# Two activation parts through one weight tile in 512 columns, with the halves added on VectorE

## The reference, cut to what matters

```
# first network, one layer
h = rms_norm(x, norm_pre_g)
proj = einsum('bsd,de->bse', h, w_in)       # q, k, u_a, z_a, o, z_b, g_a, g_b: 1024 columns each; v and gates apart
# second network, two layers; each ends with
def peer_ffn(h, w_q, sub_keys, u_tab, v_tab):
    q = (xc @ w_q).reshape(t, PEER_HEADS, 2, PEER_QDIM // 2)     # 2048 columns
    sc = einsum('thpc,hpnc->thpn', q, sub_keys)                  # then top-k, experts, sum
```

## Time and profile before

| | us |
|---|---|
| median of 3 runs (2314.62 to 2317.86) | 2315.11 |
| time of the profiled execution | 2312.29 |
| its span | 2310.5 |
| PE busy in the span | 2226.4 (96%) |
| DVE busy | 1700.3 (74%) |
| ACT busy | 1169.5 (51%) |

### The profile page before, as it was taken

One profiled execution on the slowest core, in us unless ns is written; L12 is line 12 of the kernel. 1 busy time (PEld: TensorE's weight loads), 2 busy tenths in 40 slices (PEclk: granted clock), 3 DMA queues, 4 the chain that ended last, 5 costly groups with the idle time before them and its releaser, 6 DMA issues.

```text
span 2310.5 us, 44458 instructions
## 1 busy us (share of the span) xinstructions
PE 2226.4 (96%) x15960; PEld 2011.1 (87%) x15960; DVE 1700.3 (74%) x3205; ACT 1169.5 (51%) x1688; POOL 0.2 (0%) x4
## 2 busy tenths in 40 slices
PE   7999899899999999999999998999999999999998
PEld 7998787689999999878888887899999998888886
DVE  5787676855998687798755567569977778986554
ACT  5566344545555555444444455545564554444444
POOL 0000000000000000000000000000000000000000
PEclk9999999799999999999999999999999999999999
DMA  6444244234545444455555542435554444555553
GB/s 262 178 180 152 92 149 149 73 107 149 177 169 190 156 168 168 146 172 173 183 190 190 191 153 79 155 137 173 181 179 158 172 165 149 178 166 190 190 190 137
DMA packets 95589, 376.37 MB, mean 163 GB/s; under 512 B 10861, under 2 KB 10989, under 8 KB 92817
## 3 DMA queue, kind: packets, MB, share of 16 engines
q1 hardware_dynamic: 95504, 375.29, 47.0%
HBM read 374.20 MB, written 1.05 MB: 162 GB/s over the span
## 4 chain that ended last, share of the span: by engine, by line
PE 70%; DVE 16%; ACT 2%; issue 2%; DMA 0%; ACTq 0%; SPq 0%; DVEq 0%
PE bank L328 21%; PE bank L330 21%; PE bank L329 21%; DVE tile_lo L2269 4%; PE bank L2003 3%; DVE e_hidden L2295 2%; DVE e_hidden L2289 2%; DVE e_hidden L2301 1%; DVE e_hidden L2341 1%; DVE e_hidden L2343 1%; DVE e_hidden L2339 1%; PE bank L2087 1%; DVE tile_lo L260 0%; PE bank L295 0%; PE bank L875 0%
## 5 line engine op out<-in xcount | busy, mean ns | idle before, releaser
L329 PE MATMUL bank<-a_lo,tile_hi 128*128 128x256 f32 x2688 | 756.1, 281 | 0.0
L328 PE MATMUL bank<-a_hi,tile_hi 128*128 128x256 f32 x2176 | 623.1, 286 | 16.4 <-DVE tile_lo L2269 5.3
L330 PE MATMUL bank<-a_hi,tile_lo 128*128 128x256 f32 x2176 | 613.7, 282 | 0.0
L329 PEld LDWEIGHTS bank<-a_lo,tile_hi 128*128 128x128 f32 x2688 | 511.4, 190 | 0.0
L2221 ACT ACTIVATE tile_hi<-wbuf 128x1024 fp32r<-128x1024 f32 x248 | 263.4, 1062 | 388.3 <-PE bank L330 385.4
L328 PEld LDWEIGHTS bank<-a_hi,tile_hi 128*128 128x128 f32 x2176 | 413.1, 190 | 24.1 <-issue 13.7
L2393 DVE TENSOR_TENSOR tile_lo<-wbuf,tile_hi 128x1024 fp32r<-128x1024 f32 x256 | 312.3, 1220 | 164.2 <-ACT tile_hi L2221 164.2
L330 PEld LDWEIGHTS bank<-a_hi,tile_lo 128*128 128x128 f32 x2176 | 413.3, 190 | 0.0
L328 PE MATMUL bank<-tile_hi,hidden_hi 128*128 128x512 f32 x1024 | 407.4, 398 | 5.0 <-DVE hidden_lo L2396 5.0
L330 PE MATMUL bank<-tile_hi,hidden_lo 128*128 128x512 f32 x1024 | 402.7, 393 | 0.0
L329 PE MATMUL bank<-tile_lo,hidden_hi 128*128 128x512 f32 x1024 | 402.4, 393 | 0.0
(11 more groups left out here) (355 smaller groups left out, 3112.6 us busy)
## 6 DMA issues: line engine op xcount, KB each, us to landing
wbuf<-in_peer_u SPq DMA_DIRECT2D x256, 512.0 KB, 3.5
wbuf<-in_peer_v SPq DMA_DIRECT2D x256, 512.0 KB, 3.5
wbuf<-in_w_in SPq DMA_DIRECT2D x16, 2048.0 KB, 7.7
wbuf<-in_peer_q SPq DMA_DIRECT2D x32, 512.0 KB, 4.0
wbuf<-in_hyb_in SPq DMA_DIRECT2D x16, 512.0 KB, 3.6
wbuf<-in_mla_uq SPq DMA_DIRECT2D x9, 512.0 KB, 3.5
wbuf<-in_mla_in SPq DMA_DIRECT2D x8, 528.0 KB, 3.3
wbuf<-in_w_v SPq DMA_DIRECT2D x2, 2048.0 KB, 7.2
```

The costliest lines, as they stand in the source:

```text
L328: nc.tensor.matmul(out, hi[:, cols], other_hi, start=start, stop=False, **kw)
L329: nc.tensor.matmul(out, hi[:, cols], other_lo, start=False, stop=False, **kw)
L330: return nc.tensor.matmul(out, lo[:, cols], other_hi, start=False, stop=stop, **kw)
```

## The change

In the input sections and the query projections a triple of matmuls becomes a pair. The two parts of the activations lie side by side (`n_parts`, `q_parts`, seen as 2 x 256 columns); `lo` of the weights goes with the high activations alone (256 columns), and `hi` of the weights with both parts in one matmul of 512 columns. The sum for an output tile now takes a whole bank: one half holds hi·hi + lo·hi, the other hi·lo. ACT copies the half with hi·lo out, and DVE adds the other half to it; DVE's addition is what frees the bank. In the input sections four banks are now used by groups of two, and groups alternate between two pairs of banks; in the query projections tile j uses bank 2 + j % 2, and PE waits for the kept tile j-2 before every tile from j = 2 on. `n_hi` moves to the buffer that was `a_hi`; eight semaphores are taken from the pool that is cleared and used again later. The core of it:

```
+def paired_products(nc, out, main, hi, lo, parts, other_hi, k, start, stop):
+    cols = slice(k * P, (k + 1) * P)
+    nc.tensor.matmul(out[:, main * S:(main + 1) * S], lo[:, cols], other_hi, start=start, stop=False, ...)
+    return nc.tensor.matmul(out, hi[:, cols], parts, start=False, stop=stop, skip_group_check=True)

 # input sections, PE (one triple becomes one pair; banks by twos)
-  last = three_products(nc, bank[:, b, e * S:(e + 1) * S], in_hi[:, slot, :], in_lo[:, slot, :],
-                        n_hi[:, k, :], n_lo[:, k, :], n, k == 0, k == KT - 1)
+  last = paired_products(nc, bank[:, 2 * (b % 2) + e, :], 1, in_hi[:, slot, :], in_lo[:, slot, :],
+                         n_parts[:, :, k, :], n_hi[:, k, :], n, k == 0, k == KT - 1)
 # ACT: starts bank_free at 2 instead of 4; after each group
-  nc.scalar.activation(proj[...2 tiles...], bank[:, b, :], ACT.Copy).then_inc(bank_free, 1)
+  nc.scalar.activation(proj[...2 tiles...], bank[:, 2 * (b % 2):2 * (b % 2) + 2, 0:S], ACT.Copy).then_inc(low_kept, 1)
 # DVE: after the rest of the piece that ACT rounds before that copy
+  def add_parts(i, b):
+      part = proj[:, bass.ds(i * KT + 2 * b, 2), :]
+      dve.wait_ge(low_kept, 4 * i + b + 1)
+      nc.vector.tensor_tensor(part, bank[:, 2 * (b % 2):2 * (b % 2) + 2, S:2 * S], part, ALU.add).then_inc(bank_free, 1)

 # query projections, PE
-  if j >= 4 and j % 2 == 0:
-      pe.wait_ge(q_kept, j // 2 - 1)
-  columns_product(nc, pe, g, M_Q + j, bank[:, 2 + j // 2 % 2, ...256 columns...], q_hi, q_lo, ...)
+  if j >= 2:
+      pe.wait_ge(q_kept, j - 1)
+  pe.wait_ge(lo_done, M_Q + j + 1)
+  for k in range(KT):
+      last = paired_products(nc, bank[:, 2 + j % 2, :], 0, tile_hi[:, slot, :], tile_lo[:, slot, :],
+                             q_parts[:, :, k, :], q_hi[:, k, :], k, k == 0, k == KT - 1)
 # ACT, per tile, ahead of round_tile(M_Q + j + SLOTS)
-  if j % 2:
-      nc.scalar.activation(q_T[...2 tiles...], bank[:, 2 + j // 2 % 2, :], ACT.Copy).then_inc(q_kept, 1)
+  act.wait_ge(used, M_Q + j + 1)
+  nc.scalar.activation(q_T[:, j, :], bank[:, 2 + j % 2, S:2 * S], ACT.Copy).then_inc(q_low, 1)
 # DVE
+  def keep_query(j):
+      dve.wait_ge(q_low, j + 1)
+      nc.vector.tensor_tensor(q_T[:, j, :], bank[:, 2 + j % 2, 0:S], q_T[:, j, :], ALU.add).then_inc(q_kept, 1)
   for j in range(HALVES - 1):
       ...
       rest_tile(nc, dve, g, M_Q + j + SLOTS)
+      keep_query(j)
+  keep_query(HALVES - 1)
```

More of the change, by code:

```diff
@@ L131, in build @@
         _, h_at = fixed("h_T", [P, KT, S])
-        _, other_at = fixed("h_other", [P, KT, S])
+        fixed("h_other", [P, KT, S])
         wbuf, wbuf_at = fixed("wbuf", [P, NW, SLOTS * TILE])
@@ L159, in build @@
             "tile_lo": rounded("tile_lo", [P, SLOTS, TILE], wbuf_at + 2 * BUF),
[L160 to L161 removed]
+            "a_parts": rounded("a_parts", [P, 2, KT, S], h_at),
             "hidden_hi": rounded("hidden_hi", [P, SLOTS, S], x_at),
@@ L170, in build @@
         }
+        g["a_lo"], g["a_hi"] = (g["a_parts"][:, part, :, :] for part in range(2))
         early = []
@@ L330, in three_products @@
     return nc.tensor.matmul(out, lo[:, cols], other_hi, start=False, stop=stop, **kw)
+def paired_products(nc, out, main, hi, lo, parts, other_hi, k, start, stop):
+    cols = slice(k * P, (k + 1) * P)
+    nc.tensor.matmul(out[:, main * S:(main + 1) * S], lo[:, cols], other_hi, start=start, stop=False, skip_group_check=True)
+    return nc.tensor.matmul(out, hi[:, cols], parts, start=False, stop=stop, skip_group_check=True)
 def first_layer(nc, g, ins):
@@ L343, in first_layer @@
         gate_hi, gate_lo = (g["rounded"](f"gate_{n}", [P, KT, GATES], sig_at + i * KT * GATES * 4) for i, n in enumerate(("hi", "lo")))
-        at = sb.at()
         v_one = sb("v_one", [P, NT, HEADS, HD + 1], stack=own)
-        n_hi, n_lo = g["rounded"]("n_hi", [P, KT, S], at), g["a_lo"]
+        n_hi, n_lo, n_parts = g["a_hi"], g["a_lo"], g["a_parts"]
         mix = sb("mix", [P, GROUPS, 2, 2 * P], stack=own)
@@ L517, in behind, with keep_low @@
                     if j % 4 == 3:
[L518 to L522, removed]
+                        keep_low(i, j // 4)
+                def keep_low(i, b):
+                    nc.scalar.activation(proj[:, bass.ds(i * KT + 2 * b, 2), :], bank[:, 2 * (b % 2):2 * (b % 2) + 2, 0:S],
+                                         ACT.Copy).then_inc(low_kept, 1)
                 act.wait_ge(g["in_loaded"][0], DMA)
@@ L712, in next_rest @@
                         rest(source, pieces % SLOTS_IN, pieces + 1)
+                        behind = pieces - SLOTS_IN
+                        if behind < PIECES * NSEC and behind % 4 == 3:
+                            add_parts(behind // PIECES, behind % PIECES // 4)
                         pieces += 1
@@ L1916, in expert_layer @@
     xn = flat(24, 32).rearrange("p (t d) -> p t d", t=NT)
-    q_hi, q_lo = (g["rounded"](f"{tag}_q_{n}", [P, KT, S], hidden_at + row * S * 4) for n, row in (("hi", 32), ("lo", 40)))
+    q_parts = g["rounded"](f"{tag}_q_parts", [P, 2, KT, S], hidden_at + 32 * S * 4)
+    q_hi, q_lo = (q_parts[:, part, :, :] for part in range(2))
     junk = flat(48, 56).rearrange("p (t d) -> p t d", t=NT)
@@ L2066, in tensor @@
         for j in range(HALVES):
-            if j >= 4 and j % 2 == 0:
-                pe.wait_ge(q_kept, j // 2 - 1)
-            columns_product(nc, pe, g, M_Q + j, bank[:, 2 + j // 2 % 2, (j % 2) * S:(j % 2 + 1) * S], q_hi, q_lo,
-                            None if j else parts_ready)
+            slot = (M_Q + j) % SLOTS
+            if j >= 2:
+                pe.wait_ge(q_kept, j - 1)
+            pe.wait_ge(lo_done, M_Q + j + 1)
+            for k in range(KT):
+                if j == 0:
+                    parts_ready(k)
+                last = paired_products(nc, bank[:, 2 + j % 2, :], 0, tile_hi[:, slot, :], tile_lo[:, slot, :],
+                                       q_parts[:, :, k, :], q_hi[:, k, :], k, k == 0, k == KT - 1)
+            last.then_inc(used, 1)
             if j == 6:
```

25 lines of the change are left out of this document (13 added, 12 removed).

## The result

The changed kernel is slower: 2326.62 us median of 7 runs (2322.47 to 2330.09) against 2314.46 for the kernel before in the same comparison, a ratio of 1.0057 with a 95% interval of 1.0045 to 1.0068. That is +10.4 to +15.7 us; the forecast was +7.8 and 2322.9 us, in a range of 2315 to 2331. The profiled execution took 2322.47 us (span 2320.7). The page, against the earlier trace rows: 768 matmuls fewer, 64 operations more on DVE.

What follows compares the result with a forecast made beforehand. PE's matmul count and columns bound both places, with DVE close behind in the sections. Sections -4.1, queries +10.2 and clock +1.7 sum to +7.8 us on 2315.1: 2322.9 us, range 2315 to 2331.

Steps and rivals of the forecast that it cites:

- Tile 2: Query projections: PE waits at tile 2 for tile 0's addition, which DVE reaches only after the norm; +3.4 us a layer.
- The short waits: Query projections: PE waits 0.52 us for a freed bank at tiles 4, 6, 9, 12 and 14; +2.6 us a layer.
- 2.6 - 0.9: Query projections, per layer: five stalls add 2.6 us; fourteen tiles of cheaper pairs give back 0.9.
- the term +1.7: Query projections: PE's idling ahead of tile 2 drops the clock once in two layers, costing 1.7 us (0 to +3.4).
- after 2.27 us it stayed at 1.00; 3.5 lies between: Clock: fell after 4.14 us idle, stayed up after 2.27; tile 2's 3.5 lies between, so one fall was taken.
- The pair in the sections: Input sections: a pair takes 346.5 ns against the triple's 354.6; 512 pairs save 4.1 us (0 to 6).
- In the input sections PE never waits: Input sections before the change: PE never waits while DVE is busy for 82 of 100 us.
- the prediction took 0 for it: Input sections: DVE's new additions fit within the slots' slack and cost PE 0 us, bounds 0 and +4.
- Rival 1: Sections: a pair costs its columns alone, 320 ns, saving 17.9 us; queries about +10; total 2307 us; 8%.
- Rival 2: Sections: DVE becomes the bound at 5.66 us a group against PE's 5.54; +5 on top, 2328 us; 14%.
- Rival 3: Whole kernel: the clock never falls and the pair gains 12 ns; +3.6, 2318.7 us; 15%.
- Rival 4: Queries: the order lets additions come early, so PE is not reached; only its gain of 6 is left, 2309 us; 3%.

Runs made afterwards that it cites:

- experiment 1: Kernel before with the matmul pair in the input sections only, query projections as before: 2312.0 us, ratio 0.9996 to the kernel before.
- experiment 2: Kernel before with the matmul pair in the query projections only, sections as before: 2328.13 us, ratio 1.0066 to the kernel before.
- experiment 5: Changed kernel, query additions ahead of the rests, tile 0's inside the norm's root, tile 1's right behind the normed x: 2309.12 us, ratio 0.9987 to before.
- experiment 3: Changed kernel with fourteen unused 512-column matmuls in PE's wait ahead of query tile 2: 2324.98 us, ratio 1.0045 to the kernel before.
- experiment 4: Changed kernel with DVE's addition of a query tile ahead of the rest of tile j+4: 2316.31 us, ratio 1.0015 to the kernel before.
- experiment 9: The changed kernel run once more, unaltered: 2327.06 us.
- experiment 8: Changed kernel with a 128x512 memset on DVE behind each section addition, the bank freed behind it: 2332.08 us in one execution.
- kernel 6: Experiment 5's kernel with ACT's sine of the table moved behind piece 5 of section 1: 2305.22 us, ratio 0.9972 to the kernel before.
- experiment 10: Kernel 6 run once more, unaltered: 2307.93 us.
- experiment 11: New sections and the sine behind piece 5 of section 1, with the queries of the kernel before: 2309.74 us, ratio 0.9987 to before.
- experiment 7: Kernel before with only ACT's sine moved behind piece 5 of section 1: 2311.41 us, ratio 0.9998 to the kernel before.

## Why the prediction was right, and where it was off

**The sign, the place and the mechanism were right.** Removing a matmul of three gains little, because the columns stay; the addition in DVE's written order costs more, because it sits in the loop that frees a bank. Experiments 1 and 2 put all of the loss in the queries, and experiment 5 turns it into a gain by moving the same additions.

**Tile 2** was forecast to begin 3.4 us later: it waits 3.30 us, and it begins 12.99 us after the turning of x, where it was 9.58, so 3.41 later. The chain was as written, with 0.42 us for an addition I had put at 0.45. That is also the estimate that the prediction took from the Trainium skill, "VectorE: DVE Perf Modes", section "The TRN2 errata"; 14 of them in the trace of e0 average 418 ns.

**The short waits** came where they were forecast, at tiles 4, 6, 9, 12 and 14, but smaller than the 0.52 I had: in e0 PE starts 0.30 to 0.37 us late (at tile 9 the last pair before the wait began 0.72 us earlier, where 0.35 is usual). In e1 the waits at tiles 9, 12 and 14 are the same and the first two are spread over tiles 4, 5 and 6. The tile that waited ended 3.20 after the one ahead, the other 2.88, 6.08 for the two as worked out; without waits two tiles take 5.62 (experiment 5), so a wait costs 0.46 with the restart. From the start of tile 2 to `seed(0)` e0 took 4.25 us more than before, 1.85 with the clock's 2.4 taken off, where the forecast had 2.6 - 0.9. Experiment 3, which takes the clock out, leaves 5.3 and 5.1 us a layer against 5.1.

**The clock was mis-sized: the term +1.7.** I took one fall in two layers at 1.7 us. It fell in both, and a fall cost 2.4, so +4.8. The 3.4 us at half speed came from one gap elsewhere; here the half lasted 6.8 us, 5.5 of them after PE had started again. Where a fall did last 3.4 us, its price was the 1.7 I had (experiment 4). This is 3.1 of the difference between +7.8 and the measured stretches' sum. The step "after 2.27 us it stayed at 1.00; 3.5 lies between" was weak as well: the kernel before had a fall behind a shorter wait, 1.97 us at the end of section 0 (the windows below), which I hadn't read. Idle time alone doesn't decide it here.

**The pair in the sections** gains 9.2 ns in 70 to 170 by counts and 8.9 from start to start, where I had 8, and the whole stretch shortened by 4.2 us, where I had 4.1. The terms of my sum were themselves counts, a little low: from start to start the 256-column matmul takes 118.5 ns and the 512-column one 230.3. The agreement of the whole is partly luck. Between the first matmul of the sections and the first of `v` the kernel before took 185.9 us, of which 1.97 was a wait and about 1.7 a lowered clock; the changed kernel took 181.8 with 3.17 of waits and no lowered clock. The pairs account for 182.2 - 178.6 = 3.6 us, 7 ns each (they gained 8.9 ns behind section 0 and some 2 in it), the longer wait takes 1.2 back, and the clock happened to stay up. In experiments 3, 4, 5 and 9, with the same sections and a fall, the stretch to the routing took 209.4 to 210.6 us, so the gain was 1.7 to 2.9. That may be why experiment 1's time shows so little of its trace's 4.2; how many of its executions had the fall isn't shown.

**"In the input sections PE never waits" was wrong.** I read it from the window 70 to 170 and didn't look at section 0. The kernel before, in its windows and ACT's timeline:

```profile
45.00:50.00 5.00, 3.03 (x26) 2.83 (x24) 3.77 (x11) 2.26 (x5) 0.00 (x0) 1.00 0.15 62
50.00:55.00 5.00, 5.00 (x32) 5.00 (x31) 2.04 (x5) 1.92 (x4) 0.00 (x0) 0.66 0.52 154
```

```profile
47.74 0.36 ACT L532 ACTIVATE trig<-sig 128x192 f32<-128x192 f32 x1 [3.39 <-DVE sig L683]
```

The changed kernel has the same line with a longer wait, since an addition of 0.61 us now stands among DVE's table steps, at 44.98 (and three more stand earlier in the section):

```profile
47.88 0.36 ACT L540 ACTIVATE trig<-sig 128x192 f32<-128x192 f32 x1 [4.79 <-DVE sig L698]
```

So the addition isn't free in the sections, where the prediction took 0 for it: PE waits 1.2 us more there. In four of the six traces with a wait of 2.9 us the clock fell too, for 3.4 or 6.8 us, which made the stretch up to 2.6 us longer; the kernel before has a fall of its own there, 1.7 us of work, so only the rest of that is new.

**The rivals.** Rival 1 (a pair at its columns' price) is out: 345 and 352 ns by counts, never 328. Rival 2 (DVE bounds the sections) is out for the conv sections and the pooling, but narrowly: DVE is full in the pooling, and with 0.5 us more a group PE begins to wait at the end (experiment 8). Rival 3 is out, as the clock fell. Rival 4 is out as a description of this order and right as a design: with the additions early, the change doesn't reach PE (experiment 5).

**What stays open.** Why pairs run at 352 ns in one stretch and at 345 in another, and why the same wait of 2.9 us leaves the clock up in two traces, drops it for 3.4 us in one and for 6.8 in three. What made kernel 6 faster than kernel 5. Stretches outside the change also differ by 1 to 3 us between executions, so that the medians (+12.2 us) can't be held against the sum of the traced stretches (+11.1) more closely than that.

## What to carry to other kernels

An addition that finishes a PSUM result also frees the bank, so it belongs ahead of the work that prepares the next tiles; the queries' 32 additions cost 15 us behind that work, with the clock's fall in it, and nothing ahead of it (experiments 2 and 5). Before a cost is put at nothing on a busy engine, look at the first and the last turn of the loop and not at its steady state alone: section 0 had a wait that the windows of the middle didn't show. A new long wait of PE has a second price, the lowered clock behind it; a run that fills the wait with matmuls measures it by itself, if it is read in the trace of that stretch.

## What the runs showed of the hardware

- The granted clock fell to half around waits of 1.92 us (experiments 6, 10 and 11), 1.97 (the kernel before), 2.16 (experiment 4, both layers), 3.30 (query tile 2) and 3.39 us (experiment 8), and around 2.9 us at the end of section 0 in four traces of six; it stayed up behind 0.99 (experiment 7) and 2.27 us. Idle time alone doesn't tell it. It can fall while PE waits (changed kernel, 1.3 us before tile 2) or after PE has started again (kernel before, section 0, 1.1 us after). The time at half speed was 3.4 us in some falls and 6.8 in others, and at one place (the end of section 0) both came.
- Pairs of 256 and 512 columns under one weight tile run at one of two paces, 345 or 352 ns by counts (346.7 or 353.3 from start to start), at a granted clock of 1.00 in both. The pace of section 0 and that of the sections behind it differ in six of the ten traces with pairs. The triples of 256 columns ran at 354.6 ns (355.6) in every one of the three profiles that had them.
- DVE's addition from PSUM takes 0.42 us for 256 columns, 0.34 to the next instruction, and 0.69 for 512, 0.61 to the next; ACT's copy of 256 columns 0.38, 0.28 to the next. The moving operand of 512 columns lies in two runs of 256; that showed no price of its own at the faster pace (by counts 345.4 - 118.2 = 227.2 ns, where 228.3 was expected from the earlier trace rows).
